# The first norm and first matmul block of a fused transformer kernel, in two halves of four chunks

## The reference, cut to what matters

```python
mod_l = (jax.nn.silu(c) @ w_mod[i] + b_mod[i]).reshape(b, N_MOD, 1, D_MODEL)
mod_c = (jax.nn.silu(c_ctx) @ w_mod[i] + b_mod[i]).reshape(N_MOD, 1, D_MODEL)
def modulate(x, gain, shift, scale):
    return rms_norm(x, gain) * (1 + scale) + shift
def swiglu(h, w_in, w_out):
    a, b = jnp.split(h @ w_in, 2, axis=-1)
    return (jax.nn.silu(a) * b) @ w_out
x_lat = x_lat + 0.5 * mod_l[:, 2] * swiglu(modulate(x_lat, norm_gain[i, 0], mod_l[:, 0], mod_l[:, 1]),
                                         ffn_a_in[i], ffn_a_out[i])
```

## Time and profile before

| | us |
|---|---|
| median of 3 runs | 2511.37 (2510.39 to 2513.14) |
| the profiled execution | 2512.09 |
| its span, first to last instruction | 2509.9 |
| PE busy | 2426.7 (97%) |
| DVE busy | 1403.3 (56%) |
| ACT busy | 1087.9 (43%) |
| mean granted TensorE clock | 0.990 |

### The profile page before, as it was taken

The page is one execution under the profiler, slowest core; times in us unless marked ns, Lnnn a source line. Parts: engine busy times, 40 slices in busy tenths (PEclk is TensorE's granted clock), DMA queues, the critical chain, the costliest instruction groups (busy, mean ns, idle before and its releaser), DMA issues.

```text
span 2509.9 us, 44857 instructions
## 1 busy us (share of the span) xinstructions
PE 2426.7 (97%) x17771; PEld 1571.0 (63%) x17771; DVE 1403.3 (56%) x1959; ACT 1087.9 (43%) x1621; POOL 258.5 (10%) x255
## 2 busy tenths in 40 slices
PE   6999999998999999999999999999999999999998
PEld 4444444464544444444444458888888888878887
DVE  5557443467465553275543355367766765786774
ACT  4544323245354443254433331255545555565553
POOL 1134001005100000100002201022101000010001
PEclk9999999999999999999999999999999999999999
DMA  9996532330246553345643243236886676544674
GB/s 318 194 216 211 170 97 76 92 101 17 74 145 201 186 177 110 113 152 183 201 138 103 82 126 91 62 101 190 237 242 179 199 220 175 153 135 122 195 205 133
DMA packets 621372, 384.19 MB, mean 153 GB/s; under 512 B 11179, under 2 KB 580880, under 8 KB 621128
## 3 DMA queue, kind: packets, MB, share of 16 engines
q1 hardware_dynamic: 616568, 369.27, 49.5%
q0 software_dynamic: 4112, 11.44, 3.0%
q10 hardware_dynamic: 576, 1.83, 0.2%
HBM read 381.41 MB, written 1.08 MB: 152 GB/s over the span
## 4 chain that ended last, share of the span: by engine, by line
PE 86%; DVE 7%; DMA 2%; ACT 2%; SPq 1%; issue 1%; ACTq 0%; DVEq 0%
PE PS L673 24%; PE PS L675 24%; PE PS L674 24%; DMA arena<-in_w_mod 2%; DVE WL L1697 2%; PE PS L690 2%; PE PS L692 2%; PE PS L691 2%; PE PS L625 1%; DVE arena L1947 1%; PE PS L1056 1%; DVE XL L1953 1%; ACT WH L1196 1%; SPq L515 1%; PE PS L1020 1%
## 5 line engine op out<-in xcount | busy, mean ns | idle before, releaser
L673 PE MATMUL PS<-XH,WH 128*128 128x512 f16 (+2 forms) x2912 | 942.9, 324 | 21.8 <-DVE XL L1953 11.7
L674 PE MATMUL PS<-XL,WH 128*128 128x512 f16 (+2 forms) x2912 | 942.0, 324 | 0.0
L675 PE MATMUL PS<-XH,WL 128*128 128x512 f16 (+2 forms) x2912 | 941.4, 323 | 0.0
L1196 ACT ACTIVATE WH<-W 128x1024 f16<-128x1024 f32 (+1 forms) x520 | 556.7, 1107 | 671.6 <-PE PS L675 578.9
L1697 DVE SCALAR_TENSOR_TENSOR WL<-W,WH 128x1024 f16<-128x1024 f32 (+1 forms) x520 | 669.9, 1318 | 236.9 <-ACT WH L1196 236.7
L673 PEld LDWEIGHTS PS<-XH,WH 128*128 128x128 f16 x2912 | 286.3, 98 | 209.5 <-issue 28.5
L675 PEld LDWEIGHTS PS<-XH,WL 128*128 128x128 f16 x2912 | 286.2, 98 | 179.9 <-issue 4.4
L674 PEld LDWEIGHTS PS<-XL,WH 128*128 128x128 f16 x2912 | 286.0, 98 | 169.8 <-issue 3.5
L673 PE MATMUL PS<-arena,WH 128*128 128x256 f16 (+1 forms) x1184 | 379.0, 320 | 1.9 <-DVE WL L1697 1.9
L674 PE MATMUL PS<-arena,WH 128*128 128x256 f16 (+1 forms) x1184 | 378.9, 320 | 0.0
L675 PE MATMUL PS<-arena,WL 128*128 128x256 f16 (+1 forms) x1184 | 378.9, 320 | 0.0
(11 more groups left out here) (289 smaller groups left out, 2078.8 us busy)
## 6 DMA issues: line engine op xcount, KB each, us to landing
arena<-in_w_mod SPq DMA_DIRECT2D x72, 1024.0 KB, 7.9
W<-in_ffn_a_in SPq DMA_DIRECT2D x88, 512.0 KB, 5.0
W<-in_ffn_b_in SPq DMA_DIRECT2D x88, 512.0 KB, 4.6
W<-in_w_ffn_gu SPq DMA_DIRECT2D x88, 512.0 KB, 4.2
W<-in_ret_in SPq DMA_DIRECT2D x48, 512.0 KB, 4.4
W<-in_ffn_a_out SPq DMA_DIRECT2D x32, 704.0 KB, 5.7
W<-in_ffn_b_out SPq DMA_DIRECT2D x32, 704.0 KB, 5.8
W<-in_w_ffn_down SPq DMA_DIRECT2D x32, 704.0 KB, 5.8
```

The source lines that it names most:

```text
L673: mm(dst, wh, xh, start=(kp == 0 and c == 0), stop=False, skip_group_check=True)
L674: mm(dst, wh, xl, start=False, stop=False, skip_group_check=True)
L675: return mm(dst, wl, xh, start=False, stop=(kp == g["parts"] - 1 and c == kc - 1), skip_group_check=True)
L1196: return act.activation(dst, src, ACT.Copy, scale=scale)
```

## The change

Four things. (1) SP loads the strips in the order 0, 2, 1, 3 (`FIRST_ORDER`), and weight slot 0 between the second and the third of them; `mod_drain` puts each strip where it belongs. (2) PE multiplies two strips, starts block 0, and after its chunk 3 multiplies the other two strips, then goes on with chunk 4. (3) DVE makes shift and scale columns for chunks 0 to 3 and norms these eight tiles, then the same for chunks 4 to 7. (4) The split of weight slot 1 comes behind all tiles, on ACT and on DVE; ACT copies strips 2 and 3 of the order after the first eight tiles.

```diff
--- before.py
+++ after.py
@@ -408,6 +408,7 @@
         MOD_BLOCKS = N_MOD * DC
         MOD_FIRST, MOD_EARLY = 8, 2
         STRIPS_FIRST = MOD_FIRST // 2
+        FIRST_ORDER = (0, 2, 1, 3)
         m = MOD_FIRST + MOD_EARLY
         for name, pairs in (("ffn_0a_in", FC // 2), ("ffn_0b_in", FC // 2), ("ffn_1a_in", 9)):
             g = next(x for x in GEMMS if x["name"] == name)
@@ -511,7 +512,8 @@
             mod_w = io["w_mod"].rearrange("l (c p) n -> p l c n", p=P)
 
             def mod_first_load(m):
-                src = mod_w[:, 0, 4 * (m % 2):4 * (m % 2) + 4, 512 * (m // 2):512 * (m // 2) + 512]
+                strip = FIRST_ORDER[m // 2] if m < MOD_FIRST else m // 2
+                src = mod_w[:, 0, 4 * (m % 2):4 * (m % 2) + 4, 512 * strip:512 * strip + 512]
                 sp.dma_start(M32_first[m % MOD_FIRST], src).then_inc(mod_first_loaded[m % MOD_FIRST], 16)
 
             for m in range(2):
@@ -554,9 +556,11 @@
                 n, mods = g["blocks"] // 2, g["mods"]
                 begin = 0
                 if g["w0"] == 0:
-                    for m in range(2, MOD_FIRST):
-                        mod_first_load(m)
-                    pair(0, lambda k, t: None)
+                    for k in range(2):
+                        for m in range(2 + 2 * k, 4 + 4 * k):
+                            mod_first_load(m)
+                        for t in range(2):
+                            load(g, wv, k, t, k * P + t * FF, 0)
                     for k in range(MOD_EARLY):
                         sp.wait_ge(mod_used, k + 1)
                         mod_first_load(MOD_FIRST + k)
@@ -707,6 +711,8 @@
                     elif first and g["norm"] is not None:
                         pe.wait_ge(lo_ready, 2 * w + 2)
                         for c in range(kc):
+                            if c == DC // 2 and g["w0"] == 0:
+                                first_strips(1)
 
                             tiles = 1 if g["norm"] == RET_NORM else NORMS[g["norm"]]["T"] // SEQ
                             pe.wait_ge(xl_ready, H0[g["norm"]] + c * tiles + T // SEQ)
@@ -878,16 +884,19 @@
                 for _ in range(n):
                     mm(PS[:, 3, 0:SEQ], ones, mats[:, 0:2, :].rearrange("p a b -> p (a b)"), start=True, stop=True, skip_group_check=True)
 
-            for strip in range(STRIPS_FIRST):
-                pe_mod(strip, 0)
-                if strip:
-                    keep_on(1)
-                pe_mod(strip, 1)
-                if strip == 0:
-                    pe_spread(0)
-                else:
-                    keep_on(1)
-                pe_mod_turn(strip)
+            def first_strips(half):
+                for strip in range(2 * half, 2 * half + 2):
+                    pe_mod(strip, 0)
+                    if strip:
+                        keep_on(1)
+                    pe_mod(strip, 1)
+                    if strip == 0:
+                        pe_spread(0)
+                    else:
+                        keep_on(1)
+                    pe_mod_turn(strip)
+
+            first_strips(0)
             pe.wait_ge(rel_loaded, 48)
             mm(PS[0:N_HEADS_2, 4, :], relb[:, :], onehot[0:REL_BUCKETS, :], start=True, stop=True).then_inc(rel_mm, 1)
             keep_on(3)
@@ -1415,7 +1424,7 @@
             act.wait_ge(silu_ready, 2)
             copy(silu_s[:, :, 0:2], silu_w[:, :, 0:2]).then_inc(silu_hi, 1)
             copy(silu_h[:, :, 0:2], silu_w[:, :, 0:2]).then_inc(silu_hi, 1)
-            for strip in range(STRIPS_FIRST):
+            for strip in range(2):
                 mod_copy(strip)
             begin(GEMMS[0], (0,))
 
@@ -1435,7 +1444,8 @@
                         copy(filt[:, q, :], PS[:, 4 + q % 4, :]).then_inc(filt_ready, 1)
 
             act.activation(warm[:, 0:1], mats[:, 1, 0:1], ACT.Silu)
-            act_apply(0, GEMMS[0], {2: lambda: begin(GEMMS[0], (1,))})
+            act_apply(0, GEMMS[0], {4: lambda: (mod_copy(2), mod_copy(3))})
+            begin(GEMMS[0], (1,))
 
             def run(name, **more):
                 g, after = with_next(name)
@@ -1707,7 +1717,8 @@
             def mod_drain(strip):
 
                 dve.wait_ge(mod_turned, strip + 1)
-                dve.tensor_copy(modT[:, bass.ds(4 * strip, 4), :], PS[:, 7, 0:8].rearrange("p (j s) -> p j s", j=4)).then_inc(mod_drained, 1)
+                to = FIRST_ORDER[strip] if isinstance(strip, int) and strip < STRIPS_FIRST else strip
+                dve.tensor_copy(modT[:, bass.ds(4 * to, 4), :], PS[:, 7, 0:8].rearrange("p (j s) -> p j s", j=4)).then_inc(mod_drained, 1)
 
             def mod_finish(lo, hi, norms, half, whole):
 
@@ -2035,11 +2046,37 @@
             dve.wait_ge(silu_hi, 2)
             link(tt(silu_s[:, :, 2:4], silu_w[:, :, 0:2], silu_s[:, :, 0:2], ALU.subtract))
             ts(silu_w[:, :, 0:2], silu_w[:, :, 0:2], W_SCALE, None, ALU.mult).then_inc(silu_scaled, 1)
-            for strip in range(STRIPS_FIRST):
-                mod_drain(strip)
-            mod_finish(0, MOD_FIRST, [(0, 0)], [], [])
-            split(GEMMS[0], 0, 0)
-            dve_apply(0, GEMMS[0], 5)
+
+            def first_columns(half):
+                for strip in range(2 * half, 2 * half + 2):
+                    mod_drain(strip)
+                dve.wait_ge(mod_drained, 2 * half + 2)
+                at, gain, c0 = COL[("b_mod", 0)], COL[("norm_gain", None)], 4 * half
+                for s in range(2):
+                    m, bias = (a.rearrange("p (m c) -> p m c", m=2)[:, :, c0:c0 + 4] for a in (modT[:, 0:2 * DC, s], pcol[:, at:at + 2 * DC]))
+                    ins = stt(m, m, 1.0 / W_SCALE, bias, ALU.mult, ALU.add)
+                link(ins)
+                for s in range(2):
+                    ins = stt(norm_a[:, 0, c0:c0 + 4, s], modT[:, DC + c0:DC + c0 + 4, s], 1.0, pcol[:, gain + c0:gain + c0 + 4], ALU.add, ALU.mult)
+                link(ins)
+
+            for half in range(2):
+                first_columns(half)
+                N, parts = NORMS[0], [(c, s, tok) for c in range(4 * half, 4 * half + 4) for s, tok in segs(BOTH)]
+                if half == 0:
+                    split(GEMMS[0], 0, 0)
+                    dve.wait_ge(rstd_ready, 1)
+                for i in range(len(parts) + 2):
+                    if i < len(parts):
+                        c, s, tok = parts[i]
+                        stt(N["sq"][:, c, tok], N["src"][:, c, tok], N["a"](c, s), PS[:, BANK_N + 1, tok], ALU.mult, ALU.mult)\
+                            .then_inc(h_ready, 1)
+                    if i >= 2:
+                        c, s, tok = parts[i - 2]
+                        dve.wait_ge(xh_ready, DC * half + i - 1)
+                        stt(N["l"][:, c, tok], N["sq"][:, c, tok], N["b"](c, s), N["h"][:, c, tok], ALU.add, ALU.subtract)\
+                            .then_inc(xl_ready, 1)
+            split(GEMMS[0], 0, 1)
             dve.wait_ge(rel_mm, 1)
             tt(relvec[:, :], PS[0:N_HEADS_2, 4, :], rel_mask[0:N_HEADS_2, :], ALU.add).then_inc(rel_vec, 1)
 
```

## The result

The changed kernel takes 2518.52 us (median of 10 runs, 2517.59 to 2523.52), the kernel before, measured beside it, 2513.70 (10 runs, 2509.62 to 2518.33). The ratio is 1.0020, 95% interval 1.0012 to 1.0029: the change makes the kernel slower, by 3.0 to 7.3 us. Measured once more later, the ratio was 1.0022 (1.0014 to 1.0031).

What follows compares the result with a forecast made beforehand. DVE was taken to bound the start of block 1, and so the end; handing over between DVE and PE makes it 4.0 to 4.7 us later, taken as 4.4, hence 2515.8 us against the medians, range 2511.0 to 2519.5.

Steps and rivals of the forecast that it cites:

- What bounds the kernel: DVE holds the path from 41.08 to 62.3 us; a shift of block 1's start shifts the end, within 2.1 us.
- Half 0 and the first matmul: Start of block 0: DVE's two splits end at 34.45 us and PE's first matmul comes at 37.04.
- The 24 matmuls: PE, chunks 0 to 3 of block 0: end at 44.3 to 45.0 us with a clock fall, 42.15 without.
- From there to half 1: Strips 2 and 3, drain and columns: half 1 starts 7.72 us after the 24 matmuls, at 52.0 to 52.7.
- Half 1 to `relvec`: DVE: 6.30 us of tiles, some 0.5 waiting for ACT, 2.28 for two splits; `relvec` 9.1 us after half 1.
- The hidden low clock: PE, chunks 4 to 7: a second clock fall takes up to 7.9 us but ends before DVE's first modulation split; hidden.
- The queue: SP's modulation loads behind the late second weight pair: up to 1.5 us late; taken as 0, range 0 to 1.5.
- The steady stretch: Rival, behind block 1's start: the 2.1 us of waits and the clock fall vanish; -0.2, 2511.2 us; chance 0.06.
- The signs: Right: DVE idle about 41 to 52, block 1 at about 67. Wrong: half 1 before 49 or after 55 us.
- The clock stays up: Rival, PE's wait ahead of block 0: 3.2 us does not drop the clock; +1.9, 2513.3 us; chance 0.20.
- A late queue on top of a low clock: Rival: low clock through all 24 matmuls, late modulation load stops block 2; 2518.3 to 2519.8 us; chance 0.13.
- The gain as the order of loads suggests: Rival: half 1 starts when the last strip lands, block 1 5.4 us earlier; 2506.0 us; chance 0.03.

Runs made afterwards that it cites:

- the split between the halves: Changed kernel with the split of weight slot 1 moved back among the tiles, between the two halves on ACT and DVE; ratio to before 0.9994.
- the strips after chunk 1: Changed kernel with strips 2 and 3 of the order on PE after chunk 1 of block 0 instead of chunk 3; ratio to before 1.0014.
- The filler run: Changed kernel with six more filler matmul groups ahead of block 0 and six after the second pair of strips; ratio to before 1.0015.
- filler between the blocks: Kernel with strips 2 and 3 after chunk 1, plus four filler groups on PE between block 0 and block 1; ratio to before 1.0010.
- the strips ahead: Changed kernel with strips 2 and 3 back ahead of block 0 on PE, ACT copying the third strip after four tiles; ratio to before 0.9988.
- the other hold-ups removed: Kernel with strips 2 and 3 ahead of block 0, plus earlier third-strip copy and drain, filler, and slot 1's split among half 1's tiles; 2507.92 us, ratio 0.9974.

## Why the prediction was right, and where it was not

**What bounds the kernel** held for the first part: DVE's path to `relvec` sets when block 1 can start, and the part behind block 1 did not give back more than its scatter (below). It was not the whole: the split between the halves and the strips after chunk 1 have `relvec` at T + 27.0 and T + 27.1 and ratios of 0.9994 and 1.0014. The ratios go with the turn behind block 1, in which block 1's own length counts too.

**Half 0 and the first matmul.** Forecast T + 3.38 and T + 5.97; measured T + 3.39 (37.96) and T + 5.98 (40.55). The loads in their new order cost nothing here, as forecast: no strip of the changed kernel waits for one.

**The 24 matmuls.** Forecast 7.3 to 8.0 us, measured 6.96 and 6.95. The clock did fall, as forecast, but not 2.6 us into the wait, as I had read from the earlier trace rows: it fell after PE had resumed, by 1.1 us in one trace, so that five matmuls still ran at the upper clock, and by 0.3 us in the other, and it came back 4.6 and 3.6 us after the first matmul, not 5.6. The filler run gives the price of the low clock here: 1.2 us, where the terms had 2.1 to 2.8 (44.3 to 45.0 against 42.15). The bound without a fall was too low in turn, 5.1 us against 5.75 in that run.

**From there to half 1.** Forecast 7.72, measured 7.74. **Half 1 to `relvec`.** Forecast 9.1, measured 9.0; the wait for ACT was 0.34 where I took 0.5. Its share of the loss, the late split, is shown by the run that moved it: 2.7 us. The 0.5 us of added work that I had given DVE came out as 0.1 over the kernel. Summed, `relvec` is 3.7 us later relative to T (4.5 against the second trace of before), forecast 4.0 to 4.7. The runs part it: 2.7 us are the late splits, 1.2 the low clock in the 24 matmuls, and with both removed `relvec` is at T + 25.8, level with before. The pause of DVE between the halves is thus not on top of these two: it uses up what the early start of half 0 would have gained.

**The hidden low clock.** Here a step was wrong. I let the second fall of the clock be covered by chunks 4 to 7, and asked only whether block 0 ends in time. It does. But behind it PE has a row of short waits, 1.41, 0.64, 0.73 and 0.73 us, and among them the clock fell once more and stayed low into block 1, where PE bounds the kernel: 1.3 us in the first trace, 2.6 in the second. The term had been put at nothing. The run with filler ahead of block 0 has this loss too, and the one with filler between the blocks does not. The kernel before has that loss too in one of its two traces, so how much of it belongs to the change is not settled; the two traces of each have a mean of 12.7 against 11.5.

**The queue.** Forecast: loads up to 1.5 us late, and hidden. ACT's rows of the changed kernel show the loads behind:

```profile
70.19 0.28 ACT L1205 ACTIVATE RR<-PS 128x128 f32<-128x128 f32 x1 [3.51 <-PE PS L629]
73.36 2.00 ACT L1205 ACTIVATE arena<-arena 128x1024 f16<-128x1024 f32 x2 [2.90 <-DMA arena<-in_w_mod]
76.69 2.01 ACT L1205 ACTIVATE arena<-arena 128x1024 f16<-128x1024 f32 x2 [1.33 <-DMA arena<-in_w_mod]
```

It waits 2.90 and 1.33 us for the two loads, more than I reckoned, and DVE 4.99 us for ACT. Block 2 was not held up: between block 1 and strip 5's product at 81.78 PE has no wait, and from turn to turn block 2 takes 11.60 us in both traces, before 11.59. The term was zero, as taken, but with some luck: block 1's low clock gave the loads time. With block 1 at the upper clock and the loads as late, block 2 took 0.4 us more (the strips ahead, and the filler before block 1). The steady stretch gave nothing back that could be told from scatter.

```profile
PE PS L629 <- DVE arena L1715: 3.5, 4, 1.4
PE PS L639 <- DVE modT L1721: 0.9, 1, 0.9
```

The L629 row of 3.5 is the four waits ahead of block 1; behind it stands one wait of 0.9, against 2.1 in the earlier trace rows. This wait for `modT` is a figure of chance too: the second trace of the changed kernel has one of 3.0 us, the second of before has none between block 1 and 180 us.

**The sum.** Forecast +4.4 us against the medians, measured +4.8 (3.0 to 7.3). The absolute time came out 2.7 us above the forecast of 2515.8, and 2.3 of this lies in the median of before, which with ten runs is 2513.70 instead of 2511.37. That the sum came so close is partly luck: the 24 matmuls and the wait for ACT were put some 0.5 to 1.2 us too high, and the low clock in block 1, put at nothing, came in addition.

**The signs.** Of those named, the pause of DVE between the halves and the low clock in block 0 came as said. In the first trace the times don't fit, since everything came with T 3.5 us later: half 1 started at 55.25, past the 55 that I had called a sign of being wrong, and block 1 at about 70. In the second trace they do: half 1 at 52.58, the last strip turn at 51.47, block 1 at about 67. The other sign of being wrong, a wait of PE after 70 us that grew, did show in that trace: the 3.0 us named above, where the earlier trace rows has 0.8 as the longest.

**The rivals.** "The clock stays up" did not come true in either trace; my argument for it, a wait of 2.3 us that dropped nothing, was a chance of that trace: behind the same wait of 2.29 us the strip product took 1.95 us in the second trace of the changed kernel and 3.49 in the run with the split between the halves. "A late queue on top of a low clock" names 2518.3 to 2519.8, and the measured 2518.52 lies in it, but only because the median of before moved by 2.3: its +6.9 and more is not the 4.8 measured, its condition, a low clock beyond 47 us, did not hold (it was back at 45.1, and at 41.5 in the second trace), and the queue cost nothing. "The gain as the order of loads suggests" needed PE's strips ahead of the 24 matmuls, and the two runs that put them there got 3 and 6.5 us, on both sides of its 5.4. The place of the two strips in PE's program decides between a loss and a gain: 1.0020 against 0.9988, with only ACT's copies moved beside it.

The Trainium skill, page "TensorE: Matmul & The Clock Gate", section "What's actually happening", says that the window of the activity monitor runs free of the kernel's start, so that the point at which the clock turns varies. The traces agree: with the same instructions and the same wait of 3.21 us the clock fell 1.1 us after block 0 had begun in one trace of the changed kernel and 0.3 us after it in the other, and in the two traces of the kernel before the start of the program ran once at the upper and once partly at the lower clock. What I had drawn from it, that both bounds for block 0 would turn up among executions, did not show in these two: its 24 matmuls took 6.96 and 6.95 us.

## What to carry to other kernels

Work that is put in the middle of a block to overlap it makes every instruction ahead of it in that engine's program part of its latency: here 24 matmuls stood in front of the products on which the idle engine was waiting, and the same halves with the short, awaited work first gave 3 us instead of costing 5, and 6.5 with the other hold-ups removed. When a chain is cut in two, look for the pause that arises between the parts and put the bound engine's free work (here two weight splits) into it rather than behind the last part. That a fall of the clock is hidden in one stretch settles nothing for the next: follow PE's waits up to the next stretch that it bounds.

## What was not expected of the hardware

The granted clock depends on chance more than one trace shows. In the kernel before, a wait of 2.06 us shortly ahead of the sums at 20.54 left the clock at 2.4 GHz in one execution, and one of 1.88 us ahead of those at 20.44 was followed by 1.2 GHz in the other, with T 2.7 us later. The length of this wait does not decide it: over the twelve traces the sums took 2.98 to 3.61 us behind waits of 1.75 to 2.17 us in four, and 1.95 or 1.96 us behind waits of 1.05 to 2.69 us in the other eight. And in both traces of the changed kernel the wait of 3.21 us passed at 2.4 GHz, and the fall came when PE was at work again. It falls among short waits too: in the changed kernel four waits of 0.5 to 1.4 us with bursts of 0.4 to 0.6 us between them were followed by part of block 1 at 1.2 GHz.

The time behind block 1 scatters as well. From its turn to the end of the span the twelve traces have 2434.0 us (changed, first trace: 2515.6 less 81.57) to 2440.4 (before, second: 2517.0 less 76.58), with no relation to the edit. That is why effects of 1 to 2 us show in the traces, by their distance from T, and not in the ratios. The T and block 1 of a kernel stand on one trace each, two for the kernel before and the changed one. What makes that scatter was not tried.
